# A hybrid decoder step on one core: prompt query products as three split products, first scores ahead of the latent queries, rotary key read ahead of the query norm

## The reference

```python
proj = h @ w_in                                   # 1024 -> 512 + 256 + 32
c_q  = _rmsnorm(proj[..., :512], g_q)             # query latent
c_kv = _rmsnorm(proj[..., 512:768], g_kv)         # key/value latent
k_pe = _apply_rope(proj[..., 768:], cos, sin)     # rotary key
q    = (c_q @ w_q_up).reshape(B, L, 16, 64 + 32)  # 16 heads
q_nope, q_pe = q[..., :64], _apply_rope(q[..., 64:], cos, sin)
kv   = (c_kv @ w_kv_up).reshape(B, L, 16, 64 + 64)
s    = (q_nope . k_nope + q_pe . k_pe) * scale    # causal, softmax, times v, times w_o
q_lat = einsum('bqhn,rhn->bqhr', q_nope, w_uk)    # for the 64 new columns only
```

## Time and profile before

| | us |
|---|---|
| median of 3 runs (1633.74 to 1638.12) | 1636.54 |
| the profiled execution: its own time | 1630.78 |
| its span, first to last instruction | 1629.0 |
| ahead of the pairs, 0 to 84.71 | 84.71 |
| first pair, 84.71 to 117.81 | 33.10 |
| all 8 pairs, 84.71 to 337.31 | 252.60 |
| after the pairs | 1291.69 |
| PE busy over the span | 1516.3 (93%) |

### The profile page before, as it was taken

How to read it: one execution, slowest core, us unless ns; L and a number is a source line. 1 busy time by engine, 2 the same in 40 slices (tenths; PEclk the granted TensorE clock), 3 DMA queues, 4 the chain that set the end, 5 groups by cost and what they waited for, 6 DMA issues and landing times.

```text
span 1629.0 us, 31779 instructions
## 1 busy us (share of the span) xinstructions
PE 1516.3 (93%) x11325; PEld 1419.5 (87%) x11325; DVE 765.3 (47%) x1219; ACT 594.7 (37%) x1038; POOL 342.9 (21%) x398
## 2 busy tenths in 40 slices
PE   5988888879999899999999999789999999999995
PEld 5856666659889799999999999679999999999994
DVE  3765545554555354342334454874444432344332
ACT  6333443375555333321133323442233311233321
POOL 0274564424430102210022133020012200122000
PEclk9989999899999999999999999799999999999997
DMA  7122322422332322322222375603322232222221
GB/s 174 24 60 74 93 82 71 120 85 82 98 112 68 103 79 78 90 78 90 78 78 80 102 230 124 233 15 86 87 78 77 78 91 85 76 84 78 83 61 58
DMA packets 245278, 147.56 MB, mean 91 GB/s; under 512 B 42071, under 2 KB 239614, under 8 KB 244190
## 3 DMA queue, kind: packets, MB, share of 16 engines
q1 hardware_dynamic: 238114, 139.39, 29.3%
q0 software_dynamic: 6704, 7.20, 1.8%
q10 hardware_dynamic: 396, 0.13, 0.0%
HBM read 128.42 MB, written 18.26 MB: 90 GB/s over the span
## 4 chain that ended last, share of the span: by engine, by line
PE 80%; DVE 5%; issue 5%; ACT 2%; POOL 1%; POOLq 1%; DMA 0%; SPq 0%; DVEq 0%; ACTq 0%
PE bank L852 58%; PE bank L772 5%; PE bank L965 4%; PE bank L1091 3%; PE bank L1056 3%; PE bank L915 2%; PE bank L932 1%; PE bank L978 1%; PE bank L972 1%; DVE arena_parts L1800 1%; DVE tmpa L2275 1%; ACT arena L1346 1%; DVE arena L2302 1%; DVE sq L2275 1%; PE bank L992 0%
## 5 line engine op out<-in xcount | busy, mean ns | idle before, releaser
L852 PE MATMUL bank<-arena_parts,wR 128*128 128x288 f32 x4224 | 565.1, 295 | 7.8 <-ACT arena_parts L1415 3.7
L852 PEld LDWEIGHTS bank<-arena_parts,wR 128*128 128x128 f32 x4224 | 560.7, 188 | 10.2 <-issue 6.8
L852 PE MATMUL bank<-side_parts,wR 128*128 128x288 f32 x3360 | 447.2, 295 | 1.1 <-DVE tmpa L2347 1.1
L852 PEld LDWEIGHTS bank<-side_parts,wR 128*128 128x128 f32 x3360 | 445.4, 188 | 1.5 <-issue 1.3
L1814 DVE TENSOR_TENSOR wR<-wraw,wR 128x1024 fp32r<-128x1024 f32 x159 | 232.7, 1464 | 237.9 <-ACT wR L1409 236.5
L1409 ACT ACTIVATE wR<-wraw 128x1024 fp32r<-128x1024 f32 x159 | 167.0, 1050 | 201.9 <-PE bank L852 187.5
L735 POOL TENSOR_TENSOR arena_parts<-sq,arena_parts 128x576 f32 x64 | 91.6, 1432 | 674.1 <-ACT arena_parts L1627 674.1
L1346 ACT ACTIVATE arena<-bank 128x256 f32<-128x256 f32 (+9 forms) x223 | 95.7, 445 | 155.6 <-PE bank L972 65.8
L1624 ACT ACTIVATE tmpa<-bank 128x576 f32<-128x576 f32 x64 | 41.7, 652 | 195.4 <-PE bank L852 195.4
L2198 DVE TENSOR_TENSOR sq<-tmpa 128x576 f32<-128x576 f32 x64 | 48.5, 758 | 127.1 <-ACT tmpa L1624 127.1
L772 PE MATMUL bank<-ident,arena 128*128 128x128 f32 (+4 forms) x400 | 69.2, 293 | 19.5 <-DVE arena L1980 15.4
(11 more groups left out here) (295 smaller groups left out, 1500.9 us busy)
## 6 DMA issues: line engine op xcount, KB each, us to landing
wraw<-in_mlp_w SPq DMA_DIRECT2D x128, 512.0 KB, 3.9
side<-in_cache_ckv SPq DMA_DIRECT2D x128, 128.0 KB, 2.1
wraw<-in_ssm_w_glu SPq DMA_DIRECT2D x16, 512.0 KB, 3.9
s_state_to_out<-side SPq DMA_DIRECT2D x16, 256.0 KB, 2.5
s_in_to_state<-yblk SPq DMA_DIRECT2D x8, 512.0 KB, 2.6
s_in_to_out<-side SPq DMA_DIRECT2D x64, 64.0 KB
wraw<-in_mla_w_o SPq DMA_DIRECT2D x8, 512.0 KB, 5.2
side<-s_in_to_state SPq DMA_DIRECT2D x2, 2048.0 KB, 12.7
```

Source lines behind the costliest of these rows:

```text
L852: return pe.matmul(bank[:, a, 0:HALF], wR[:, s, wp, k, :], tokens(k, xp)[:, a * HALF:(a + 1) * HALF], start=(first and j == 0), stop=(last ...
```

## The change

Three edits:

1. The query products become split products. ACT writes the query latent straight into `cqH` (float32r); DVE writes its rest (`rest_of_latent`) and frees the bank afterwards. ACT cuts the pair's weights out of the raw loads, swapped strips included (`cut_queries_of`, six instructions, `wq_hi`), for pair 0 ahead of the pairs and for pair p+1 inside pair p, behind the exponential of unit 3; POOL subtracts to get the rests (six instructions, `wq_lo`) in place of its two copies. The raw weights and the rests lie in idle slots of `wraw` and `wR`, so their first load waits until blocks 0 to 4 have been cut, and three loads of `w_o` wait for the last query product.
2. PE makes the scores of units 0 and 1 ahead of the latent queries; DVE takes their maxima ahead of copying the latent queries out.
3. DVE reads the rotary key out of PSUM ahead of the query norm; PE's wait for that norm's reciprocal moves behind the query products of the pair (`var_ready`).

ACT's loop now covers 7 pairs, and the last is written out.

```diff
             def pair_weights(p):
                 for h in range(2):
-                    sp.dma_start(wq[:, :, h, 0:HD], w_qup[...]).then_inc(hw_in, 16)
+                    sp.dma_start(wq_raw[h], w_qup[...]).then_inc(hw_in, 16)
...
+            sp.wait_ge(w_hi, 5)
+            sp.wait_ge(w_lo, 5)
             pair_weights(0)
...
             first_pages(PAIRS - 1)
+            sp.wait_ge(q_done, 2 * PAIRS)
             for m in (0, 1, 3):
                 load_block(B_B + m, col(w_o, 0, m))
...
-            pool.wait_ge(blk_done, B_B)
             with pool.Fori(0, PAIRS) as p:
-                pool.wait_ge(hw_in, p * 96 + 96)
+                pool.wait_ge(wq_hi, p + 1)
                 apart(pool)
-                pool.tensor_copy(wq[:, :, :, 96:112], wq[:, :, :, 80:96]).then_inc(hw_swap, 1)
-                pool.tensor_copy(wq[:, :, :, 112:128], wq[:, :, :, 64:80]).then_inc(hw_swap, 1)
+                for h in range(2):
+                    for to, at, n in ((0, 0, HD), (96, 80, 16), (112, 64, 16)):
+                        pool.tensor_tensor(wqL[:, :, h, to:to + n], wq_raw[h][:, :, at:at + n],
+                                           wqH[:, :, h, to:to + n].bitcast(F32), ALU.subtract).then_inc(wq_lo, 1)
+                pool.wait_ge(blk_done, B_B)
...
             with pe.Fori(0, PAIRS) as p:
                 pe.wait_ge(hw_in, p * 96 + 96)
-                pe.wait_ge(hw_swap, p * 2 + 2)
+                pe.wait_ge(wq_lo, p * 6 + 6)
                 for h in range(2):
                     for a in range(2):
-                        for k in range(4):
-                            ins = pe.matmul(pair[h][:, a, 0:HALF], wq[:, k, h, :], cqT[:, k, a * HALF:(a + 1) * HALF],
-                                            start=(k == 0), stop=(k == 3))
+                        cols = slice(a * HALF, (a + 1) * HALF)
+                        for j, (w, x) in enumerate(((wqH, HI), (wqH, LO), (wqL, HI))):
+                            for k in range(4):
+                                ins = pe.matmul(pair[h][:, a, 0:HALF], w[:, k, h, :], cqH[:, k, cols] if x == HI else cq_lo[k][a],
+                                                start=(j == k == 0), stop=(j == 2 and k == 3))
                     ins.then_inc(q_done, 1)
                 pe.wait_ge(h_ready, H_CKV + 2)
+                pe.wait_ge(var_ready, 2)
...
                 ins.then_inc(uk_done, 1)
+                pe.wait_ge(qn_sb, p * 2 + 2)
+                pe.wait_ge(qr_sb, p * 2 + 2)
+                pe.wait_ge(k_sb, p * 2 + 2)
+                pe.wait_ge(kpe_raw, 1)
+                unit_scores(p, 0)
+                unit_scores(p, 1)
                 pe.wait_ge(uk_sb, p + 1)
-                pe.wait_ge(qn_sb, p * 2 + 2)
...
                 ins.then_inc(ql_done, 1)
-                pe.wait_ge(qr_sb, p * 2 + 2)
-                pe.wait_ge(k_sb, p * 2 + 2)
-                pe.wait_ge(kpe_raw, 1)
-                unit_scores(p, 0)
-                unit_scores(p, 1)
...
+            def cut_queries_of(p):
+                act.wait_ge(hw_in, p * 96 + 96)
+                for h in range(2):
+                    for to, at, n in ((0, 0, HD), (96, 80, 16), (112, 64, 16)):
+                        ins = act.activation(wqH[:, :, h, to:to + n], wq_raw[h][:, :, at:at + n], ACT.Copy)
+                ins.then_inc(wq_hi, 1)
...
+            cut_queries_of(0)
             root(1)
...
                     if u + 2 < 8:
                         unit_exp(p, u + 2)
+                    if u == 1 and not last:
+                        cut_queries_of(p + 1)
...
+            def rest_of_latent(r):
+                dve.wait_ge(cq_hi, r + 1)
+                dve.wait_ge(w_lo, (4, 5, 7, 7)[r])
+                for a in range(2):
+                    ins = dve.scalar_tensor_tensor(out=cq_lo[r][a], in0=in_banks[(r + 2) % 3][:, a, 0:HALF],
+                                                   scalar=vecs[:, V_Q + r:V_Q + r + 1],
+                                                   in1=cqH[:, r, a * HALF:(a + 1) * HALF].bitcast(F32),
+                                                   op0=ALU.mult, op1=ALU.subtract)
+                ins.then_inc(tile_free, 1)
...
             add_square(Q_CQ + 3, 1)
+            rest_of_latent(3)
             dve.wait_ge(h_ready, 2)
-            latent_rstd(1, QL_D)
...
             tt(halves(tmpa[64:96, 1, :]), bank[96:128, :, 0:HALF], halves(ropek[96:128, :]), ALU.mult)\
                 .then_inc(tile_free, 1)
-            settle()
+            latent_rstd(1, QL_D)
...
+                unit_max(p, 0)
+                unit_max(p, 1)
                 dve.wait_ge(ql_done, p + 1)
...
-                unit_max(p, 0)
-                unit_max(p, 1)
```

More of the change, by code:

```diff
@@ L120, in build @@
         hT = sb("hT", [P, KT, N])
-        wraw = sb("wraw", [P, RAW, 8, P])
+        wraw, wrawR = sb_with_parts("wraw", [P, RAW, 8, P], [P, RAW * 8 * P], F32R)
         wR = sb("wR", [P, CUT, 2, 8, P], F32R)
@@ L151, in build, with cut_view @@
         in_arena = view
+        flat_z = zR.rearrange("p m a n -> p (m a n)")
+        def cut_view(n):
+            view(n)
+            return flat_z[:, offset[0] - n:offset[0]]
         ckvT = view(2 * N).rearrange("p (r n) -> p r n", r=2)
@@ L157, in build @@
         flat_c = view(2048)
+        cq_tail = flat_z[:, offset[0] - HALF:offset[0]]
         CN = flat_c.rearrange("p (b n) -> p b n", b=DEC_B)
@@ L160, in build @@
         mark = offset[0]
-        cqT = view(4 * N).rearrange("p (r n) -> p r n", r=4)
+        cqH = cut_view(4 * N).rearrange("p (r n) -> p r n", r=4)
         qT = view(2 * N).rearrange("p (h n) -> p h n", h=2)
@@ L164, in build @@
         V = view(BLK * P).rearrange("p (t n) -> p t n", t=BLK)
-        wq = view(4 * 2 * P).rearrange("p (k h n) -> p k h n", k=4, h=2)
+        wqH = cut_view(4 * 2 * P).rearrange("p (k h n) -> p k h n", k=4, h=2)
+        wqL = wR[:, 1].rearrange("p a k n -> p (a k n)")[:, 0:1024].rearrange("p (k h n) -> p k h n", k=4, h=2)
+        wq_raw = [wraw[:, s].rearrange("p k n -> p (k n)")[:, N:N + 4 * HD].rearrange("p (k n) -> p k n", k=4) for s in (0, 3)]
+        cq_lo = [[wrawR[:, at + HALF * a:at + HALF * a + HALF] for a in range(2)] for at in (3 * 1024, 0, 2 * 1024, 2 * 1024 + N)]
+        cq_lo[3][1] = cq_tail
         wkv = view(2 * 2 * P).rearrange("p (r c h n) -> p r c h n", r=2, c=2, h=2)
@@ L172, in build @@
         SW = PAST + DEC_Q
-        flat_z = zR.rearrange("p m a n -> p (m a n)")
-        def cut_view(n):
-            view(n)
-            return flat_z[:, offset[0] - n:offset[0]]
         KP3 = cut_view(PAGES * 3 * ROPE).rearrange("p (g z n) -> p g z n", g=PAGES, z=3)
@@ L289, in build @@
         nat_done, nat_sb = sem("nat_done"), sem("nat_sb")
-        hw_in, hw_swap = sem("hw_in"), sem("hw_swap")
+        hw_in, wq_hi, wq_lo, cq_hi = sem("hw_in"), sem("wq_hi"), sem("wq_lo"), sem("cq_hi")
         q_done, qn_sb, qr_sb = sem("q_done"), sem("qn_sb"), sem("qr_sb")
@@ L465, in pair_weights @@
                 for h in range(2):
-                    sp.dma_start(wq[:, :, h, 0:HD], w_qup[:, :, ds(p * (2 * HD) + h * HD, HD)]).then_inc(hw_in, 16)
+                    sp.dma_start(wq_raw[h], w_qup[:, :, ds(p * (2 * HD) + h * HD, HD)]).then_inc(hw_in, 16)
                 for r in range(2):
@@ L1442, in _ @@
                 else:
-                    act.activation(halves(cqT[:, m - 2, :]), src, ACT.Identity,
-                                   scale=vecs[:, V_Q + m - 2:V_Q + m - 1]).then_inc(tile_free, 1)
+                    act.activation(halves(cqH[:, m - 2, :]), src, ACT.Identity,
+                                   scale=vecs[:, V_Q + m - 2:V_Q + m - 1]).then_inc(cq_hi, 1)
                 if m < 2:
@@ L1491, in chunk_turned, with pair_of_heads @@
                     copy(bbD[rows, :, :, GS * half:GS * half + GS], bb[rows, :, ds(p * QC, QC), :]).then_inc(bbD_sb, 1)
-            with act.Fori(0, PAIRS) as p:
+            def pair_of_heads(p, last):
                 act.wait_ge(k_done, p + 1)
@@ L1507, in _ @@
                 heads_out(p)
+            with act.Fori(0, PAIRS - 1) as p:
+                pair_of_heads(p, False)
+            pair_of_heads(PAIRS - 1, True)
             for j in range(BLK):
@@ L1913, in _ @@
             add_square(Q_CQ, 0)
+            rest_of_latent(0)
             powers(2)
@@ L1916, in _ @@
             add_square(Q_CQ + 1, 1)
+            rest_of_latent(1)
             dve.wait_ge(const_in, 16 * 4)
@@ L1935, in _ @@
             add_square(Q_CQ + 2, 0)
+            rest_of_latent(2)
             dve.wait_ge(rstd_ready, 1)
```

## The result

The changed kernel takes **1619.24 us** (median of four runs, 1617.70 to 1621.41); the kernel before, in the same job, 1635.14 (four runs, 1633.50 to 1638.12). The ratio is 0.9907, with an interval of 0.9884 to 0.9931: faster by 0.7 to 1.2%. The forecast was 1618.0.

The account below looks back on a forecast made before the run. No engine is full; a pair is a chain from engine to engine, and only time on it counts. 7 × 2.18 = 15.3 plus 3.2 for the first pair, 18.5 off 1636.5, gives 1618.0 us, range 1608 to 1627.

Parts of the forecast that it names:

- Query products: PE at each pair's start: 48 split matmuls instead of float32 ones, 8.03 to 6.63 us, 1.40 off each pair.
- Scores ahead of the latent queries: PE and DVE before the first reciprocal: scores come 1.87 us earlier, DVE hands 1.09 back waiting, 0.78 gained a pair.
- Rival B: Only the query products gain; a wait on ACT or DVE fills what the reorder frees: 11.6 us off, 1625, chance 0.14.
- The pair: Each later pair, first scores to softmax: 30.8 to 28.6 us, first reciprocal 13.1 us after its start instead of 15.3.
- a pair above 29.5, or a clock below 0.94 in most pairs: Signs in the pairs' profile, in us and granted PE clock, that would say the prediction is wrong.
- Rival A2: PE's clock: every pair gets the seventh's long lower-clock stretch, 18.6 us lost, total 1636.5, chance 0.07.
- ACT's cut and its load: Behind unit 3's exponential: six instructions, 1.74 to 2.5 us, no cost (bad end 0.7 a pair), load 0.4 ahead.
- rival C: ACT waits between exponentials for late loads of the next pair's weights: 5 us slower, 1642, chance 0.05.
- POOL: Six subtractions for weight rests in each pair: at most 3.3 us instead of 0.6, hidden in its idle time, no cost.
- Ahead of the pairs: DVE's eight added instructions cost nothing, at worst 1.6 us; early rotary key gains 1.8; PE starts near 82.
- The sum: Whole kernel: 7 × 2.18 = 15.3 for later pairs plus 3.2 for the first, 18.5 us off.
- Rival A1: PE's clock: the lower-clock stretches go, 7 × 1.6 + 3.1 = 14 us more gained, total 1604, chance 0.14.

Follow-up runs that it names:

- x1: The changed kernel with scores and maxima of units 0 and 1 put back behind the latent queries (old order): 1616.57 us, ratio 0.9899 to before.
- x2: The kernel before with only the new order of scores and maxima, query products still float32: 1628.9 us, ratio 0.9968.
- x9: The kernel before plus eight unread PE products ahead of the first two transposes of probabilities in each pair: 1624.6 us, ratio 0.9955.
- x10: The changed kernel with the old order of scores, plus eight unread PE products ahead of the first two transposes of probabilities: 1616.0 us, ratio 0.9896.
- x8: The changed kernel again, without an edit, in a later job: 1615.24 us, ratio 0.9903 to before.
- x4: The changed kernel with ACT's cut of the next pair's weights behind unit 5's exponential instead of unit 3's: 1618.01 us, ratio 0.9908.
- x5: The changed kernel plus eight unread PE products a pair, ahead of the first two transposes of probabilities: 1605.85 us, ratio 0.9846.
- x3: The changed kernel plus eleven unread PE products a pair, three ahead of the latent queries, eight ahead of the first two transposes: 1609.3 us, ratio 0.9851.
- x6: The changed kernel plus eleven unread PE products a pair behind the query products, where PE has no gap: 1624.38 us, ratio 0.9948.

## Why the prediction held, and where it was off

The time came out as forecast, 1619.24 for 1618.0, faster as said. By its steps:

*Query products.* Predicted 8.03 to 6.63, 1.40 a pair. Both lengths run to the modelled end of the last matmul, and by this measure the 48 take 153.41 + 0.70 − 147.49 = 6.62 here; from start to start it is 6.46 for 7.86. Both ways it is 1.4. Between before and x1, without a stretch, the first reciprocal (15.27 to 13.97) and the period (29.68 to 28.38) gain 1.30 of it. Right. (The estimate of 5.88 by the Trainium skill, "TensorE: Matmul & The Clock Gate", section "Back-to-back issue gap", whose formula is for an isolated matmul, was 0.58 below the 6.46.)

*Scores ahead of the latent queries.* Predicted 0.78 and not 1.87, since DVE would wait for the latent queries. DVE does wait, 1.14 us, and the order is worth 0.60 (x2 against before) and 0.5 to 0.7 (the changed kernel against x1). Right in its mechanism, 0.1 to 0.3 too much. Rival B, that it gains nothing, falls as a statement on the chain. In the medians no gain shows: x1, without the order, is as fast within the interval.

*The pair.* Predicted 30.8 to 28.6, its first reciprocal at 13.1. The first reciprocal came at 13.26 and the gain without lower clock is 29.68 − 27.8 = 1.9 instead of 2.18. But the prediction also said that a pair above 29.5, or a clock below 0.94 in most pairs, would prove it wrong, and the profiled execution shows just that: 30.6 at 0.89. The step that failed is the one that moved the old rows by 2.18 and left the clock as it was. The stretches became twice as long, 6.8 us for 3.4, and what they cost was 19.6 us in this execution, for 12.0 in that of before. With the new order alone (x2) the long ones come too, and with the old order (x1, x9, x10) 3.4 us is the rule; why the order does this is not shown. The prediction also misread where a stretch begins: not behind the gaps around the latent queries, which the change narrows, but three microseconds later, behind the wait ahead of the first transposes, which it leaves. Rival A2, that every pair gets the long stretch of the seventh, was right in kind and too large: 6.8 us and not 10.2, and not in every execution: x8's cost, 11.4, is below that of before. Its price for a 3.4 us stretch, 1.6 us, was too high: in x1 one costs 1.1.

*ACT's cut and its load.* Predicted 1.74 to 2.5 us, at no cost, the load landing 0.4 ahead. It takes 1.52, and it starts at 163.19, right behind the accumulator read of 163.10, with no wait on a transfer; rival C didn't come. x4 finds nothing to gain from moving it.

*POOL.* Predicted at most 3.3 us; it takes 3.06, behind 8.83 us of waiting.

*Ahead of the pairs.* Predicted nothing, at worst 1.6 us: the last block moved by 0.35. DVE's first scaling was to come 1.8 us earlier and came 1.5 earlier, about this 0.35 less. PE was to start near 82, with POOL's rests, and started at 83.58, on them: POOL began them at 80.47 and not at 78.81, as four of its products ahead of them had taken 5.57 us instead of 4.26. To the first reciprocal the first pair gained 2.55 and, in x8, 2.99, for 3.2 predicted.

*The sum.* Predicted 3.2 + 7 × 2.18 = 18.5, at an unchanged clock. The chain gave 2.55 to 2.99 and 7 × 1.9 = 13.3, thus about 16.0. The medians differ by 15.9 in both jobs, 2.6 less than the sum. That the forecast is only 1.2 us off is partly luck: its base, 1636.5, was a median of three runs, and with the fourth it is 1635.14.

That the clock didn't spoil the total is luck too, since the prediction set its change at nothing because the rows spoke for neither side. For the first trace 2.55 + 13.2 (7 × 1.88) − (19.6 − 12.0) = 8.1, the shift of the last pair's end; for x8 2.99 + 13.2 + (12.0 − 11.4) = 16.8, where the ends differ by 334.43 − 317.69 = 16.7. These sums close by construction, as the cost of the clock is what is left over. What is not by construction is that this remainder fits the stretches that were counted, at prices from other traces: before, seven at 1.1 and one at 4.2 (both x1) make 11.9, for 12.0; after, seven at 2.9 (x2) make 20.3, for 19.6; in x8 four make 11.6, for 11.4. So the clock's term swings by 8 us between two executions of the same program.

If the chain gave 16.0 and the medians 15.9, the clock cost about the same before and after on the median, since the stage behind the pairs keeps its length within 2.5 us (1293.1 to 1295.6 in the six traces of the table). That is argued; no trace of a median execution shows it. The executions' mean clock can't decide it: it is lower after the change (0.966 for 0.969 on average in x8's job), but it covers the stage behind the pairs too, where it is 0.98 before and 0.97 after at nearly the same length.

The same account, with the same remainder, for x1: 3.36 + 7 × 1.30 + (12.0 − 7.5) = 17.0, and 334.43 − 317.47 = 17.0. It gives up 4 us of chain, and its stretches cost less. And x5: 2.43 + 7 × 1.58 + 12.0 = 25.5, against 25.8.

Rival A1 put the time without any stretch at 1604. The changed kernel doesn't get there by itself; with eight unread products it does, at 1605.85, which is faster than both kernels (0.9846 of before, interval below 0.9880; the changed kernel in the same job 0.9903, from 0.9875 on, so the two intervals overlap by 0.0005; all four of its executions, 1605.35 to 1608.22, are below all six of x8, from 1612.50 on).

The Trainium skill, "TensorE: Matmul & The Clock Gate", section "Why this matters for your kernels", warns of gaps in PE's work that bring the lower clock back. In kind x3, x5 and x6 agree: such products help in the gap and not outside it. In size they differ: the gaps that the page names are longer than any of PE's in these pairs (1.37 us at most, before and after), and the lower clock came all the same.

## What to carry to other kernels

Sum a chain at one clock and keep the clock as a term of its own: cut windows to the stretches at the lower level, read what a pair costs with and without one, and compare the totals only after that. An edit that shortens the chain can look worthless (the order here), and undoing it can look free, when it only changes how long those stretches last. Where PE waits on a handover in each round, a few products that nobody reads, put into that wait and not elsewhere, are worth a try: here they cost some 0.3 us of a round and saved up to 2.9. In the old order the same products did not keep the clock in all pairs, so try each place with a trace.

## What the runs showed of the hardware

- Stretches at the lower clock came in lengths of 3.4, 6.8 and 10.2 us and cost a pair 1.1, 2.9 and 4.2 us (29.5 in x1, 30.6 in the changed kernel and 32.6 in x1, against 28.38, 27.7 and 28.38). The first 3.4 us cost less than the next: in x2, 3.4 us cost 1.07 and 6.8 cost 2.9.
- In the traces of before and of the changed kernel, stretches of neighbouring pairs start 30.7 to 30.8 us apart (before from 103.0 at 133.8, 164.5 and 195.2; after from 100.8 at 131.6, 162.3 and 193.0), about as long as a pair with a stretch of 3.4 or 6.8 us lasts there, 30.6 to 30.8. There the hits come in runs; why is not shown.
- How many pairs were hit differs between executions of one program: seven stretches in the first trace of the changed kernel and four in x8's. The spread of the runs goes with it: of x8's six executions the fastest took 1612.50 us at a mean granted clock of 0.969 and the slowest 1622.70 at 0.963, and of the fourteen of before beside them 1627.50 at 0.974 and 1636.81 at 0.964.
- DVE's addition of two 32x576 halves takes 0.75 us in the third pair of the changed kernel and 1.54 (L2032 at 95.31) in the first, while POOL runs its chunk products; in x4, which moves those, 1.68 to 1.75 in the fourth and fifth. The Trainium skill, "SBUF — State Buffer", section "Who interferes with whom", has a DVE instruction with two SBUF inputs contend with a GpSimd instruction that reads SBUF; these rows agree. DVE's instructions of 576 columns with one input from PSUM took 0.75 and 0.76 in both places.
